# Differential attention: scores over a full 128-row contraction, and the next head's sums of squares taken earlier, with their roots in one batch

## What is computed

```python
q = rms_norm_2(q.reshape(B, S, H, 2, d), qn_g)          # d = 64, H = 8
k = rms_norm_2(k.reshape(B, S, H, 2, d), kn_g)
...
s = einsum("bhmqd,bhmkd->bhmqk", qblk, kt) * scale + bias   # bias = -slope * distance, causal
p = softmax(s, axis=-1)
a = p[:, :, 0] - lam * p[:, :, 1]
o = einsum("bhqk,bhkd->bhqd", a, vt)
...
o = rms_norm_2(o, subln_g) * (1.0 - lambda_init)
```

## Time and profile before

| | |
|---|---|
| median of 3 runs | 1371.56 us (1370.57 to 1371.70) |
| the profiled execution's own time | 1372.26 us |
| its span, first to last instruction | 1370.4 us |
| TensorE busy | 1253.2 us (91%) |
| VectorE, ScalarE busy | 844.4 us (62%), 591.8 us (43%) |
| mean granted TensorE clock | 0.970 of 2.4 GHz |
| HBM | 91 GB/s over the span |

### The profile page before, as it was taken

One profiled execution on the slowest core, in us unless ns is written; L12 is line 12 of the kernel. 1 busy time (PEld: TensorE's weight loads), 2 busy tenths in 40 slices (PEclk: granted clock), 3 DMA queues, 4 the chain that ended last, 5 costly groups with the idle time before them and its releaser, 6 DMA issues. The chain is left out here.

```text
span 1370.4 us, 17211 instructions
## 1 busy us (share of the span) xinstructions
PE 1253.2 (91%) x6574; PEld 1031.4 (75%) x6582; DVE 844.4 (62%) x1406; ACT 591.8 (43%) x1076; POOL 19.1 (1%) x36
## 2 busy tenths in 40 slices
PE   5979989888695999999999999999998899999998
PEld 4979867776595897777777766788776688588888
DVE  4785676656644223787778786688566665573341
ACT  6534445434443344565565555332554222462220
POOL 2000000000000000000000000000000000000001
PEclk9989999999898899999999999999999999999999
DMA  9874211110033121221212213222211323132321
GB/s 344 293 262 145 79 62 47 47 47 16 16 124 131 54 93 62 77 62 35 73 63 77 77 46 124 92 92 91 79 62 39 131 68 107 41 108 77 97 88 47
DMA packets 33074, 125.92 MB, mean 92 GB/s; under 512 B 3840, under 2 KB 4096, under 8 KB 32480
## 3 DMA queue, kind: packets, MB, share of 16 engines
q1 hardware_dynamic: 29520, 107.49, 23.7%
q0 software_dynamic: 3184, 17.01, 3.4%
q10 hardware_dynamic: 288, 0.31, 0.1%
HBM read 118.51 MB, written 6.29 MB: 91 GB/s over the span
## 5 line engine op out<-in xcount | busy, mean ns | idle before, releaser
L403 PE MATMUL bank<-hl,wh 128*128 128x512 f32 x880 | 368.1, 418 | 9.9 <-ACT th L945 4.7
L405 PE MATMUL bank<-hh,wh 128*128 128x512 f32 x880 | 347.7, 395 | 0.0
L404 PE MATMUL bank<-hh,wl 128*128 128x512 f32 x880 | 347.2, 394 | 0.0
L1480 DVE TENSOR_TENSOR wl<-raw,wh 128x1024 fp32r<-128x1024 f32 x179 | 214.6, 1223 | 117.3 <-ACT wh L917 115.2
L917 ACT ACTIVATE wh<-raw 128x1024 fp32r<-128x1024 f32 x179 | 184.3, 1054 | 221.0 <-PE bank L405 198.3
L403 PEld LDWEIGHTS bank<-hl,wh 128*128 128x128 f32 x880 | 168.1, 191 | 51.7 <-issue 16.3
L405 PEld LDWEIGHTS bank<-hh,wh 128*128 128x128 f32 x880 | 167.6, 190 | 37.5
L404 PEld LDWEIGHTS bank<-hh,wl 128*128 128x128 f32 x880 | 168.4, 191 | 35.9 <-issue 5.8
L1857 DVE SCALAR_TENSOR_TENSOR ca<-u,vt,ca 128x512 f32<-128x512 f32 x232 | 157.9, 744 | 0.0
L403 PE MATMUL bank<-wl,hh 128*128 128x256 f32 (+1 forms) x352 | 103.3, 293 | 6.2 <-DVE cumt L1567 3.8
L404 PE MATMUL bank<-wh,hl 128*128 128x256 f32 (+1 forms) x352 | 101.6, 289 | 0.0
(11 more groups left out here) (286 smaller groups left out, 1984.0 us busy)
## 6 DMA issues: line engine op xcount, KB each, us to landing
raw<-in_chunks SPq DMA_DIRECT2D x203, 512.0 KB, 3.7
x<-in_x POOLq DMA_DIRECT2D x4, 512.0 KB, 10.5
mem_scratch<-kvm POOLq DMA_DIRECT2D x1, 2048.0 KB, 6.8
x<-in_x POOLq DMA_DIRECT2D x1, 2048.0 KB, 8.6
x_scratch<-x POOLq DMA_DIRECT2D x1, 2048.0 KB, 6.5
kvm<-mem_scratch POOLq DMA_DIRECT2D x1, 2048.0 KB, 8.2
x1r<-x_scratch POOLq DMA_DIRECT2D x1, 2048.0 KB, 8.7
out_x<-x1r POOLq DMA_DIRECT2D x8, 256.0 KB, 2.5
```

Source lines behind the costliest of these rows:

```text
L403: pe.matmul(o, a[0], b[1], start=start, stop=False, **kw)
L404: pe.matmul(o, a[1], b[0], start=False, stop=False, **kw)
L405: return pe.matmul(o, a[0], b[0], start=False, stop=stop, **kw)
L1480: dve.tensor_tensor(wl[:, w], raw[:, NRAW[nxt] % RAWS], wh[:, w].bitcast(F32), ALU.subtract)\
```

## The change

Three things change in the differential stage.

1. Scores contract over 128 rows. The queries go to `qz` (for each m one tile with the other half's rows zero, which block 1 has already cleared), the keys to a new buffer `kd`, double-buffered by head. `kd` lies over `x` and `xT`, so ScalarE waits for block 1's result to be stored.
2. `total` of the next head's queries moves to tt = 1, of its keys to tt = 2, each behind four pieces. ScalarE copies each mean out of PSUM at once (`mean_of`), ahead of that tile's exponentials.
3. `roots_together` takes one logarithm and one exponential over all three rows of `norms`. It stands at tt = 2 behind the tanh of `gb`, ahead of `diff_pt_hi` and `split_v`.

The splits become three instructions in place of two on each of ScalarE and VectorE, the keys' first.

```diff
@@ TensorE
-                    three(o, (qh[half, q_], ql[half, q_]), (kh[half, 0:w], kl[half, 0:w]), True, False)
+                    three(o, (qz[:, m, 0, q_], qz[:, m, 1, q_]), (kd[:, j % 2, 0, 0:w], kd[:, j % 2, 1, 0:w]), True, False)
...
-                    for i in range(2):
-                        pieces(fill, at + min(2, half // 2) * i, min(2, half // 2))
-                        if tt == 3 and j < 7:
-                            pe.wait_ge(s.squared, 4 + 2 + 2 * j + i + 1)
-                            total(("dns", 2 * j + 2 + i), [norms[:, i, :]], blocks)
+                    pieces(fill, at, min(4, half))
+                    if tt in (1, 2) and j < 7:
+                        pe.wait_ge(s.squared, 4 + 2 + 2 * j + tt)
+                        total(("dns", 2 * j + 1 + tt), [norms[:, tt - 1, :]], blocks)
@@ ScalarE
+            def mean_of(key, dst, n):
+                banks.wait_full(act, key)
+                banks.empty(act.activation(dst, ps[7][:], ACT.Identity, scale=1.0 / n, bias=eps6), key)
+            def roots_together(keys, rows):
+                for key in keys:
+                    banks.wait_empty(act, key)
+                logs[0] += 1
+                act.activation(rows, rows, ACT.Ln).then_inc(s.logged, 1)
+                act.wait_ge(s.logged, logs[0])
+                act.activation(rows, rows, ACT.Exp, scale=-0.5).then_inc(s.rms_done, 1)
+            def split_head(j, last_scores):
+                act.activation(kd[:, j % 2, 0, :], qf[:, 1, :], ACT.Copy).then_inc(s.q_hi, 1)
+                banks.wait_full(act, last_scores)
+                for m in range(2):
+                    half = slice(HD * m, HD * m + HD)
+                    act.activation(qz[half, m, 0, :], qf[half, 0, :], ACT.Copy).then_inc(s.q_hi, 1)
...
+                    if tt == 1 and j < 7:
+                        mean_of(("dns", 2 * j + 2), norms[:, 0, :], HD)
+                    if tt == 2 and j > 0:
+                        mean_of(("sub", j - 1), rs, P)
+                    if tt == 2 and j < 7:
+                        mean_of(("dns", 2 * j + 3), norms[:, 1, :], HD)
                     if tt == 3:
                         if j < 7:
                             act.wait_ge(s.qn_done, 2 * j + 4)
-                            for i in range(2):
-                                split_q(i, qf[:, i, :], ("D", u_, 1))
+                            split_head(j + 1, ("D", u_, 1))
...
                     if tt == 2:
                         banks.empty(tanh_of(("gb", j)), ("gb", j))
                         th_free[0] = ("ga", j)
-                        act.activation(warm, eps6, ACT.Ln)
+                        roots_together(([("sub", j - 1)] if j else []) + ([("dns", 2 * j + 2 + i) for i in range(2)] if j < 7 else []),
+                                       norms[:, 0 if j < 7 else 2:3 if j else 2, :])
                     if u_ > 0:
                         diff_pt_hi(u_ - 1)
                     if tt == 2:
                         split_v(dv[:, :, j * P:j * P + P], ("DO", j - 1) if j else ("PO", 15))
-                        roots_of(*([(("sub", j - 1), rs, P)] if j else []),
-                                 *([(("dns", 2 * j + 2 + i), norms[:, i, :], HD) for i in range(2)] if j < 7 else []))
                         ahead(("gb", j))
@@ VectorE
+                    if tt == 3 and j < 7:
+                        split_keys(j + 1)
                     if tt == 3:
                         key = ("ga", j)
...
                     if tt == 3 and j < 7:
-                        for i in range(2):
-                            split_q(i, Q1 + 2 * (j + 1) + i + 1, qf[:, i, :])
+                        split_queries(j + 1)
```

More of the change, by code:

```diff
@@ L124 @@
     "h_tmp": "chunks scaled and shifted", "dve_step": "VectorE's own steps", "sumsq": "rows of squares summed",
-    "ms_done": "mean squares of block 1's tail", "sqrt_done": "their roots", "rms_done": "1 / rms taken on ScalarE",
+    "ms_done": "mean squares of block 1's tail", "sqrt_done": "their roots", "logged": "logarithms of mean squares", "rms_done": "1 / rms taken on ScalarE",
     "nk_done": "memory tiles normalised", "xn_done": "token tiles normalised (x, then x1)",
@@ L321, in build @@
             [("u", [P, C, PAD + S], F32)])
[L322 removed]
+        cos, sin, gzb, rot, sel, x, xT, kd, y = shared([("cos", [P, S], F32), ("sin", [P, S], F32), ("gzb", [P, 4, S], F32),
                                                ("rot", [P, P], F32), ("sel", [P, 8, P], BF16)],
                                               [("x", [P, T, D], F32)],
[L325 removed]
+                                              [("xT", [P, C, S], F32)], [("kd", [P, 2, 2, S], F32R)],
+                                              [("y", [P, C, S], F32)])
         cst = sb("cst", [P, K_BLOCKS])
@@ L673, in diff_scores @@
                 if tt == 0:
-                    pe.wait_ge(s.q_lo, Q1 + 2 * j + 2)
+                    pe.wait_ge(s.q_lo, Q1 + 3 * j + 3)
                 for m in range(2):
                     b = 2 + 2 * (u_ % 2) + m
-                    half = slice(HD * m, HD * m + HD)
                     banks.open(pe, b, ("D", u_, m))
                     o = ps[b][:, 0:w]
-                    three(o, (qh[half, q_], ql[half, q_]), (kh[half, 0:w], kl[half, 0:w]), True, False)
+                    three(o, (qz[:, m, 0, q_], qz[:, m, 1, q_]), (kd[:, j % 2, 0, 0:w], kd[:, j % 2, 1, 0:w]), True, False)
                     pe.matmul(o, slopes[:, j, :], dist[:, S - w:S], start=False, stop=True)
@@ L748, in x_scores @@
                 if pr == 0:
-                    pe.wait_ge(s.q_lo, Q1 + 16 + 2 * h + 2)
+                    pe.wait_ge(s.q_lo, Q1 + 24 + 2 * h + 2)
                     pe.wait_ge(s.memk_lo, h + 1)
@@ L928, in roots_of @@
                     rms[0] += 1
+                    roots[key] = rms[0]
+            logs = [0]
+            def mean_of(key, dst, n):
[8 more added lines that the diff above has]
+                act.activation(rows, rows, ACT.Exp, scale=-0.5).then_inc(s.rms_done, 1)
+                rms[0] += 1
+                for key in keys:
                     roots[key] = rms[0]
@@ L1241, in _ @@
                     act.wait_ge(s.qn_done, 2)
-                    for i in range(2):
-                        split_q(i, qf[:, i, :], ("S", UNITS - 1))
+                    act.wait_ge(s.x1_out, 16)
+                    act.wait_ge(s.zeroed, 1)
+                    split_head(0, ("S", UNITS - 1))
             def of_copy(j):
@@ L1286, in _ @@
                         key = (("dq", "dk")[tt], j + 1)
-                        raw_q(key, tt, Q1 + 2 * j + 2)
+                        raw_q(key, tt, Q1 + 3 * j + 3)
                         banks.wait_empty(act, key)
@@ L1341, in diff_tail @@
                 for i in range(2):
-                    raw_q(("xq", i), i, Q1 + 16)
+                    raw_q(("xq", i), i, Q1 + 24)
                 x_squares(0)
@@ L1363, in _ @@
                     if pr == 0 and h < 3:
-                        raw_q(("xq", 2 * h + 2), 0, Q1 + 16 + 2 * h + 2)
+                        raw_q(("xq", 2 * h + 2), 0, Q1 + 24 + 2 * h + 2)
                     if (h, pr) == (3, 0):
@@ L1380, in _ @@
                     if pr == 0 and h < 3:
-                        raw_q(("xq", 2 * h + 3), 1, Q1 + 16 + 2 * h + 2)
+                        raw_q(("xq", 2 * h + 3), 1, Q1 + 24 + 2 * h + 2)
                         x_squares(h + 1)
@@ L1818, in split_q, with split_keys, split_queries @@
                    .then_inc(s.q_lo, 1)
+            def split_keys(j):
+                dve.wait_ge(s.q_hi, Q1 + 3 * j + 1)
+                dve.tensor_tensor(kd[:, j % 2, 1, :], qf[:, 1, :], kd[:, j % 2, 0, :].bitcast(F32), ALU.subtract)\
+                   .then_inc(s.q_lo, 1)
+            def split_queries(j):
+                for m in range(2):
+                    half = slice(HD * m, HD * m + HD)
+                    dve.wait_ge(s.q_hi, Q1 + 3 * j + 2 + m)
+                    dve.tensor_tensor(qz[half, m, 1, :], qf[half, 0, :], qz[half, m, 0, :].bitcast(F32), ALU.subtract)\
+                       .then_inc(s.q_lo, 1)
             def norm_q(i, gain, key, r=None):
@@ L1835, in _ @@
                 if g == 3:
-                    for i in range(2):
-                        split_q(i, Q1 + 1 + i, qf[:, i, :])
+                    split_keys(0)
+                    split_queries(0)
             taps_done = [0]
@@ L1977, in x_split @@
                 for i in range(2):
-                    split_q(i, Q1 + 16 + 2 * h + i + 1, qf[:, i, :])
+                    split_q(i, Q1 + 24 + 2 * h + i + 1, qf[:, i, :])
                 dve.wait_ge(s.memk_hi, h + 1)
```

## The result

The changed kernel takes 1379.24 us (median of 7 runs, 1376.27 to 1382.74), the old one 1371.56 us beside it (7 runs). The ratio is 1.0063 with a 95% interval of 1.0047 to 1.0078: by the ratio 8.6 us slower, between 6.4 and 10.7 (the two medians differ by 7.7). The forecast was 1376.6 us, slower by 5.0, for the reason that the batch's delay more than eats what TensorE gains. The profiled execution took 1382.74 us (span 1381.0).

A forecast was written before the change was run, and what follows sets the result against it. TensorE bounds the old stage; afterwards the batch's delay on ScalarE and VectorE makes it wait. Terms +4.6, -1.8, +0.8, +0.6 and +0.8 give +5.0 us: 1377.3 profiled, 1376.6 median; own range 1372 to 1381, stated range 1367 to 1382.

The forecast's parts named there:

- its two waits: New TensorE waits per head: 1.3 us at the next head's scores for VectorE's split, 1.9 us at the moved total.
- Scores: 128-row score pairs on TensorE save 0.45 us each at both widths, 1.8 us a head, 14.4 us in all.
- rival 2: TensorE stays the bound because VectorE's and ScalarE's chain hides: about -15 us, some 1357 us; chance 0.12.
- Batch: At tt = 2 on ScalarE: two table loads of 1.28 us, two activations of 1.50 us, `diff_pt_hi` starting at 9.08.
- Rival 3: Only one table load for the batch's logarithm and exponential, chain 1.28 us shorter: -2.7 us, some 1369 us; chance 0.07.
- Rivals 4 and 5: Batch activations cheaper, towards 1.06 us each (some 1372 us, chance 0.13), or dearer, towards 1.89 (some 1381, chance 0.08).
- TensorE would reach the next scores at 18.21: Time after a head's point when TensorE gets to the next scores; it then waits 1.3 us, until 19.55.
- The period, +0.93 us a head: Point to point a head takes 42.49 us against 41.56; it holds five times, head 1 to head 6: +4.6 us.
- The edges: Outside the five periods: head 0 -1.8 us, totals and pairs ahead +0.8, stage's first scores +0.6, head 7 +0.8.
- The bound of rival 2: Test for TensorE staying the bound: no wait at the moved total, and the kernel is faster.

The follow-up runs named there:

- Experiment 3: Changed kernel with the batch of roots moved behind `diff_pt_hi` and `split_v` and the early table load put back: 1363.13 us, ratio 0.9947 to the old kernel.
- experiment 6: Changed kernel with the batch between `diff_pt_hi` and `split_v` and the early table load put back: 1387.70 us, ratio 1.0114 to the old kernel.
- experiment 1: Changed kernel keeping only the 128-row scores and three splits; totals, means and roots as in the old kernel: 1370.83 us, ratio 0.9999 to the old kernel.
- experiment 4: Changed kernel with VectorE's split of the keys moved behind its reading of the convolution's input: 1382.23 us, ratio 1.0085 to the old kernel.
- experiment 2: Changed kernel with 64-row scores and the old splits; moved totals, copied means and batch kept: 1382.94 us, ratio 1.0094 to the old kernel.
- experiment 9: Changed kernel with nine unused 512-column matmuls ahead of the first piece of heads 2 to 7: 1382.78 us, ratio 1.0079 to the old kernel.

## Why the prediction was right, and what in it was not

The sign and the mechanism hold: the batch holds VectorE's queue at `ptl`, behind which everything up to the next head's scores stands, and TensorE runs out of work. Experiment 3 moves the batch (and puts the early table load back) and turns 8.6 us of loss into some 7 of gain (by the ratios); experiment 6, with that load too, shows that it is VectorE's queue. But the forecast had called itself wrong if either of its two waits was missing, and as it placed them both are: the first is not there, and the second is 0.25 us where it is there at all, and not 1.9. That the length of a plain head came out within 0.16 us in spite of it is in part luck: an error of +1.0 us and one of -0.9 cancel (below).

- **Scores.** A pair of width 512 takes 2.00 us (the last matmul before it at 631.71, the first behind it at 633.94, less a step of 0.23) where 2.05 was forecast and 2.50 before: 0.50 saved a pair, not 0.45. Head 0, where nothing waits, went from 41.00 to 38.97 us: 2.0, where 1.8 was forecast. With the old order of roots the middle heads could use only 0.05 us of it (experiment 1); the prediction took the whole gain as given only for rival 2.
- **Batch.** `pth` starts 9.04 us after the head's point (forecast 9.08), the 1,536-column activations take 1.49 us (1.50), the loads 1.28. Rival 3 (one load) is out: 8 loads on line 944. Rivals 4 and 5 are out with the duration. The Trainium skill says in "ScalarE: Activation LUTs", section "Table sets: the hidden batching unit", that a logarithm and then an exponential need one load. The trace does not agree: each of the eight batches has a load of 1.28 us between them.
- **The two waits of TensorE: right in size, wrong in place.** The step that failed is that TensorE would reach the next scores at 18.21 and wait there until 19.55. There is no wait at the scores. At the moved total, where the forecast had 1.9 us, it is some 0.25 us in a head without a clock fall and none in one with. TensorE is stopped earlier, at the first piece, since the projections have two banks only and one is still full of `ga` until VectorE's line 1937, which is queued behind `norm_q` and the keys' split. I had listed the banks and not asked which is still held. In a head without a clock fall the bank waits are 2.34 + 0.60 us (head 3; 1.75 + 1.18 in experiment 4), 2.9 in sum, with the 0.25 at the total 3.2, against 1.3 + 1.9 = 3.2 forecast. The sum agrees because a head's waits are its length less TensorE's work, and both of these were nearly right; it says nothing of where TensorE stands.
- **The period, +0.93 us a head: under-sized.** From head 1's point to head 6's, the old kernel takes 207.67 us and the changed one 216.23: +8.56, where +4.6 was forecast. The parts: a plain head is 42.65, 0.16 longer than the forecast 42.49, +0.8 (the next scores start 20.59 us behind the point, 687.57 less 666.98, and not 19.55; what follows them is 0.9 us shorter than forecast, since less is waited there). Twice VectorE has one instruction more in the chain, the addition that closes a channel group's 31 taps (635.85 above, 0.69 us): +0.65 and +0.38, 1.0 us, hidden before and on the path now: the heads that have it are longer by this in experiment 4, where no fall of the clock is mixed in (43.29 and 43.03 against 42.65). The falls of the clock: 216.23 less 214.28 of experiment 4, +1.95. And 0.13 us by which the old kernel's five heads are below 5 x 41.56. 0.8 + 1.03 + 1.95 + 0.13 = 3.91, which with 5 x 0.93 = 4.65 makes the 8.56.
- **The edges.** From the stage's first scores to head 1's point 57.97 became 56.76 us, -1.2 (forecast -1.8 + 0.8 = -1.0; the rest is the pairs' 0.05 each). The wait before the stage's first scores: 2.59 against 1.88, +0.7 (forecast +0.6; experiment 2, which has no third split, keeps 1.88). From head 6's point to the last value product, head 7's: 58.36 to 59.57, +1.2 (forecast +0.8); the wait for `ptl` on the way is 2.62 against 1.65. The stage in all: +9.3 against +5.0. The ratio says +8.6 and the medians +7.7.
- **The bound of rival 2** ("none at the moved total, and the kernel is faster") was badly put: there is next to no wait at the moved total (0.25 us at most), and the kernel is slower. What decides is any wait of TensorE in the loop.
- **Not settled:** the two profiled executions differ by 10.6 us of span: 9.3 in the stage, 2.2 ahead of it and -0.9 behind. Outside the stage single profiled executions differ by as much without a reason in the program: the changed kernel's own two by 1.8 us ahead of it (first scores at 523.28 and 521.46), all versions with 128-row scores from 520.6 to 524.4 there. So the last microseconds of the account have no owner. Why the clock falls behind a wait of 2.34 us at 770.22 and not behind one of 2.34 us at 684.08 can't be told from these runs.

## What to carry to other kernels

Before a batch is placed, look at what is queued on the *other* engines behind the instruction that it delays: here 4.3 us (a logarithm, a table load and an exponential, 1.49 + 1.28 + 1.49) put ahead of a short copy that VectorE waits for cost more than every gain of the change, and the same work two places further down on ScalarE gave 0.5% instead. Where an engine is about to get slack, ask also which banks and buffers its next work opens and who still holds them; that is where it will stop. And rare instructions that were hidden (here one addition in two heads of five) count once the engine that they run on sets the pace.

## What was not expected of the hardware

TensorE's granted clock fell from 2.4 to its lower level of 1.2 GHz for some 3.4 us behind four of the six waits for `u` ahead of heads 2 to 7 (2.35, 2.99, 2.72 and 2.34 us, but not behind the other two of 2.34 and 2.72), and before it rose again matmuls of 512 columns followed each other after 0.43 us and not 0.23. Windows of the changed kernel:

```profile
590.00:600.00 10.00, 7.65 (x30) 5.74 (x30) 9.94 (x15) 4.51 (x9) 0.00 (x0) 0.87 0.17 52
640.00:650.00 10.00, 9.07 (x39) 7.49 (x40) 9.80 (x20) 4.95 (x14) 0.00 (x0) 0.83 0.18 52
```

The local loss is 1.6 us (from TensorE's restart to the scores 640.93 to 646.05, 5.12 us, against 3.53 in the same head of experiment 9), but the head is only 0.5 us longer. Head 5 (with a fall) beside head 3 (without) shows why: behind the fall it is 1.6 us late; the wait for the other bank is gone, which makes up 0.86, and the one at the moved total, 0.25. With unused matmuls in the wait the falls of these heads were gone (experiment 9), and so they were where the wait was split in two (experiment 4) and, with 64-row scores, where it was 1.2 to 1.9 us (experiment 2). In experiments 4 and 9 a fall in head 7 took the gain.
